# A fused two-block transformer kernel: the first step of both MLPs' down product as seven half-size products, and other row statistics at the border into block 3

## The chip, the cores and the metric

One core of a Trainium2 chip runs the whole kernel in one launch. The metric is the device time of one execution in microseconds (us). Engines: TensorE (PE) multiplies, ScalarE (ACT), VectorE (DVE) and GpSimd (POOL) work on elements, SyncE (SP) issues most DMAs. Each engine takes its instructions in the written order and waits on semaphores.

## The reference, cut to what matters

512 tokens of width 1024 in float32 go through two layers (sparse attention, then gated linear attention, each followed by an MLP) and a third block ("block 3": attention beside an mLSTM, then a gated feed-forward part with adaptive scale and shift). What the change touches:

```python
h = layer_norm(DN_ALPHA * h + mix, ln_mix_g[i], ln_mix_b[i])
h = layer_norm(DN_ALPHA * h + squared_relu_mlp(h, mlp_w_up[i], mlp_w_down[i]), ln_mlp_g[i], ln_mlp_b[i])
# squared_relu_mlp(x, w_up, w_down) = square(relu(x @ w_up)) @ w_down, hidden width 4096
# block 3 begins with modulate(rms_norm(x, norm_mix_g), sh1, sc1) @ w_in
```

## The kernel before, in words

**Precision.** A float32 operand is split into a high half (a rounded copy, `fp32r`, made by ScalarE) and a low half (the difference, made by VectorE, for five chunks by GpSimd). A product is three matmuls: high x high, high x low, low x high.

**Weights** come as chunks of 1 MB into three raw buffers, in the order that `weight_plan` writes; a chunk's halves go to one of the slots 0 to 3. `high(i)` on ScalarE (L1487) waits for the landing and for the last reader of the slot; `low(i)` on VectorE (L2252) waits for `high(i)`. SyncE fetches a chunk when the one three before it has been read (`released`). In between lie 24 conditioning chunks ("ada", 1 MB each), of which VectorE only forms a weighted sum (L2235 for the first of eight, L2238 for the others); the table `ADA` says how many follow each weight of each step. A `Cursor` per engine makes chunks ahead; on VectorE the weight next to a conditioning chunk goes first.

**An MLP** has eight blocks of 512 hidden units. Block n: two up weights, each giving two hidden tiles (128 units x 512 tokens), `gemm_T` (L765 to L767), 96 matmuls; ScalarE takes relu (L1629) and square (L1632) into `rb`. The down product of block n-1 follows the up product of block n. From block 1 on it is a `fold` (L960 to L962): tokens and output columns are halved, and seven products P1 to P7 of half size take the place of eight, 84 matmuls. Their operands are four quadrants of `rb`: P1, P2, P4 take them as they are (P4 the one of hidden tiles 2 and 3, second half of the tokens), the other four take sums that GpSimd makes in place (`hidden_sums`, L3407 to L3415), once the low halves of P1, P4, P2 exist. ScalarE copies each (`high_of`, L1619), VectorE makes the low half (`low_half_of`, L2437). The weights are X (left columns), Z (right), and two that VectorE sums up in the raw buffers (`weight_sums`, L2451 to L2456, and `last_weight_sum`, L2464): Y and W. TensorE's order is P1, P2, P6, P5, P7, P4, P3; P1 and P2 use X, P6 and P4 use Y, P5 uses W, P7 and P3 use Z. P1, P6, P7 are one chain in a PSUM bank, added to `h` on the way (`added`, L2477); P4 and P5 stay in four banks of their own through all steps and are added once (`lasting`); the right lower corner is corrected by the left one before and after (`corner`, L2504).

**Block 0's down product** is a plain one (`down_first`, L986 to L988, 96 matmuls) with its own operand copies (L1645, L2522), and its add also scales `h` by ALPHA (L2513). Beside it VectorE applies the layer norm's gain and shift to the four row tiles, eight pieces (`affine`, L2353).

The queues of the first MLP step of VectorE, as written:

```python
for i in range(4):      # low half of hidden tile i, then affine piece i
    ...
for q in range(2):      # low half of an up weight, then two affine pieces
    ...
cur.take(low)
low_half_of(key, 1, P4)
down_first(0)
```

**The border into block 3** (after the second MLP): TensorE runs block 7's down product by rows (L789 to L791) and, in the middle of the last row, turns rows 0 and 1 (L807); then four `queries` products (L1280 to L1282), with rows 2 and 3 turned in between (L825). VectorE adds each row (L2425), takes `bn_stats` (L2295) and `bn_aggr` (L2906), centres and multiplies by the gain (L2909), scales and shifts (L2915); ScalarE squares the result and takes a root (L1589, L1592), scales it (L1607), and copies the turned quarters (L1530); VectorE splits them (L2288, L2284).

Of the kernel before, what the change touches and what calls it, by code (L numbers as in the profile page):

```python
# [14 lines left out]
P = 128  # L15
# [11 lines left out]
ADA = {0: [(0, 0, 0), (1, 0, 1), (1, 0, 1), (1, 0, 1), (1, 0, 1), (1, 0, 1), (1, 1, 1), (1, 1, 1)],  # L27
       1: [(0, 0, 0), (1, 1, 1), (0, 0, 1), (0, 0, 1), (0, 0, 1), (0, 0, 1), (0, 0, 1), (0, 0, 0)]}
# [176 lines left out]
def weight_plan(a_w_in, a_w_o, b_w_in, b_w_o, mlp_w_up, mlp_w_down, w_ada_2, w_in_2, w_out_2, w_gate_2, w_up_2, w_down_2):  # L205
# [65 lines left out]
    def plan_mlp(i):  # L271
        plan_up(i, 0)
        slots(2, 3, 0, 1)
        plan_up(i, 1)
        for c in range(2):
            plan(mlp_w_down[i], 0, 4, c * 512, 512)
            plan_adas((ADA[i][1][2] + 1 - c) // 2)
        for n in range(2, 8):
            own = 0 if n % 2 else 2
            slots(own, 3)  # L280
# [62 lines left out]
def program(nc, x, positions, a_w_in, a_w_o, b_w_in, b_w_a2, b_b_a, b_g_norm, b_w_o, ln_mix_g, ln_mix_b,  # L343
# [4 lines left out]
    with ctx:  # L348
# [110 lines left out]
        pool_low = (5, 6, 7, 8, 9)  # L459
# [112 lines left out]
        STEPS = {"m1": (1, 6), "m2": (1, 6), "m3": (0, 3)}  # L572
# [16 lines left out]
        def freed(key, d, s):  # L589

            if key == "m3" and (d == 0 or d == 1 and s == P4):
                return s_gemm.at(("o3", T - 1, 1))
            if key != "m3" and d == 1:
                return s_gemm.at((key, "u read", 0)) if s in FIRST else s_gemm.at(None)
            return s_gemm.at((key, "P", d - 2, s, 1)) if s == P4 else s_gemm.at((key, "P", d - 1, s, 1))
# [97 lines left out]
        def tensor_program(pe):  # L693
# [82 lines left out]
            def panel_row(key, hi, lo, k0, ready, nk, first, i, t, cs=(0, 1), amid=None):  # L776
                for c in cs:
# [6 lines left out]
                    for k in range(nk):  # L784
                        if amid and (c, k) == (1, nk // 2):
                            amid()
# [187 lines left out]
            def down_first(key):  # L974
                for c in range(2):
                    i = cur.take(skip)
                    H, L, nk, ncol = parts(i)
                    w.wait_ge(*low_of(i))
                    w.wait_ge(*s_xlow.at((key, "u", 0)))
                    for t in range(T):  # L980
                        name = ((key, "down", 0), t, c)
                        o = bank[banks.take(name)][:, :]
                        w.wait_ge(*banks.free(name, s_act.sem))
                        for f in range(4):
                            X, Y = (v[:, FIRST[f], t * P:(t + 1) * P] for v in (UH4, UL4))
                            pe.matmul(o, X, H[:, f, :], start=f == 0, stop=False)  # L986
                            pe.matmul(o, X, L[:, f, :], start=False, stop=False)
                            step = pe.matmul(o, Y, H[:, f, :], start=False, stop=f == 3)  # L988
                        step.then_inc(*s_gemm.up(name, *([("chunk", i)] if t == T - 1 else [])))
                s_gemm.mark((key, "u read", 0))  # L990

            def mlp(key, x_key):
                for n in range(1, 8):
                    for q in range(2):
                        gemm_T((key, "up", n, q), x_key)
                    if n == 1:
                        down_first(key)
                    else:
                        fold(key, n - 1)
# [254 lines left out]
            def turn_first():  # L1254
                for t in range(2):
                    turn_row("x4", t, xn(t), s_act.at(("xn", t)))
# [203 lines left out]
        def scalar_program(act):  # L1460
# [137 lines left out]

            def roots_next(key):
# [21 lines left out]
            def mlp(key):  # L1621
                def relu(n, q, j):
                    i = 2 * q + j
                    w.wait_ge(*s_gemm.at(((key, "up", n, q), j)))
                    if n == 1:
                        w.wait_ge(*s_xlow.at((key, "u4", 0, i)))
                    elif n > 1:
# [14 lines left out]
                for i in range(4):  # L1642
                    relu(0, i // 2, i % 2)
                    w.wait_ge(*s_act.at((key, "square", 0, i)))
                    act.activation(UH4[:, FIRST[i], :], rb[:, i, :], ACT.Copy).then_inc(*s_xhigh.up((key, "u", 0, i)))  # L1645
                for q in range(2):
                    cur.take(high)
                    relu(1, q, 0)
                    relu(1, q, 1)
                cur.take(high)  # L1650
                high_of(key, 1, P4)
                high_of(key, 1, P1)
                high_of(key, 1, P2)
                cur.take(high)
                for n in range(2, 8):
# [22 lines left out]
                    else:  # L1678
# [3 lines left out]
                        last_high(2)  # L1682
                        weights(q1)
                        last_high(3)
# [529 lines left out]
        def vector_program(dve):  # L2214
# [251 lines left out]
            def mlp(key, x_key, n_gb):  # L2466
                last = {(t, c): ((key, "down", 0), t, c) for t in range(T) for c in range(2)}
# [5 lines left out]
                def into(t, c, ps, name):  # L2473
# [3 lines left out]
                    dve.tensor_tensor(hv, hv, ps, ALU.add).then_inc(*s_row.up(name, ((key, "down", 6), t, c)))  # L2477
# [21 lines left out]
                def corner(t, op, name):  # L2499

                    hv = h[:, t, 512:1024]
                    w.wait_ge(*s_row.at(last[t, 0]))
                    w.wait_ge(*s_row.at(last[t, 1]))
                    dve.tensor_tensor(hv, hv, h[:, t, 0:512], op).then_inc(*s_row.up(name, ((key, "down", 6), t, 1)))  # L2504
                    last[t, 1] = name

                def down_first(c):
                    for t in range(T):
                        name = ((key, "down", 0), t, c)
                        hv = h[:, t, c * 512:(c + 1) * 512]  # L2510
                        w.wait_ge(*s_gemm.at(name))
                        w.wait_ge(*s_row.at((x_key, "h", t)))
                        dve.scalar_tensor_tensor(hv, hv, ALPHA, bank[banks.of[name]][:, :], ALU.mult, ALU.add).then_inc(*s_row.up(name))  # L2513
                        banks.read[name] = s_row.at(name)
# [5 lines left out]
                for i in range(4):  # L2520
                    w.wait_ge(*s_xhigh.at((key, "u", 0, i)))
                    dve.tensor_tensor(UL4[:, FIRST[i], :], rb[:, i, :], UH4[:, FIRST[i], :].bitcast(F), ALU.subtract).then_inc(  # L2522
                        *s_xlow.up((key, "u4", 0, i), (key, "u", 0)))
                    affine(x_key, i, n_gb)
                for q in range(2):
# [3 lines left out]
                cur.take(low)  # L2529
                low_half_of(key, 1, P4)  # L2530
                down_first(0)
                low_half_of(key, 1, P1)
                low_half_of(key, 1, P2)
                cur.take(low)
                down_first(1)
                owed()
# [1116 lines left out]
```

## Time and profile before

| | us |
|---|---|
| median of 3 runs | 1813.71 (1813.1 to 1814.01) |
| the profiled execution | 1814.24, its span 1812.4 |
| TensorE busy | 1780.1 (98%) |
| VectorE, ScalarE, GpSimd busy | 1279.4, 860.4, 251.6 |
| mean granted TensorE clock | 0.998 of full |

Times in the rows below are us from the start of the span, durations are us in timelines and ns where a column says mean ns. A matmul row's 0.39 us is its whole way through the array; the next one starts after 0.227 us. A number in brackets is the engine's idle time before the instruction, and behind it what it waited for.

### The profile page before, as it was taken

What the parts mean: (1) busy time and instruction counts of PE and PEld (TensorE: products, weight loads), DVE (VectorE), ACT (ScalarE), POOL (GpSimd) and SP (SyncE); (2) the same over time, 40 slices, a digit from 0 to 9 for tenths busy, and PEclk for the clock granted to TensorE, in tenths of its full rate; (3) what the DMA queues carried; (4) which work ended last, traced back from release to release, by engine and by line L of the source; (5) the groups of instructions that cost most, each with busy time, mean ns of one, the idle gap of its engine ahead of it and who ended that gap; (6) DMA issues with size and microseconds to landing.
All of it is one profiled execution on the core that took longest, in us unless ns stands there. A gap on an engine that the chain in (4) does not pass through costs nothing.

```text
span 1812.4 us, 22763 instructions
## 1 busy us (share of the span) xinstructions
PE 1780.1 (98%) x8948; PEld 1452.2 (80%) x8948; DVE 1279.4 (71%) x2069; ACT 860.4 (47%) x1340; POOL 251.6 (14%) x188
## 2 busy tenths in 40 slices
PE   9999999999999999999999999999999999999998
PEld 7775788888888888878888888778756898888886
DVE  4997566987788578476777776987667645564774
ACT  4548453454444543555444544465466453332333
POOL 0241101111210054000111111000012001110101
PEclk9999999999999999999999999999999999999999
DMA  6220404544444122141543334232201422421331
GB/s 218 70 70 31 157 24 163 185 140 139 163 167 160 47 70 70 47 144 42 186 139 116 117 120 136 71 95 93 70 25 60 139 70 70 139 73 67 116 117 47
DMA packets 120059, 189.35 MB, mean 104 GB/s; under 512 B 7800, under 2 KB 72536, under 8 KB 116880
## 3 DMA queue, kind: packets, MB, share of 16 engines
q1 hardware_dynamic: 118416, 182.81, 30.6%
q0 software_dynamic: 1392, 4.82, 0.8%
q8 instruction: 71, 1.16, 0.3%
q14 instruction: 36, 0.29, 0.0%
q10 hardware_dynamic: 144, 0.26, 0.0%
HBM read 185.72 MB, written 2.16 MB: 104 GB/s over the span
## 4 chain that ended last, share of the span: by engine, by line
PE 84%; DVE 10%; ACT 4%; issue 2%; DMA 0%; DVEq 0%; ACTq 0%
PE bank L767 11%; PE bank L765 11%; PE bank L766 11%; PE bank L960 6%; PE bank L962 6%; PE bank L961 6%; PE bank L739 3%; PE bank L741 3%; PE bank L740 3%; PE bank L1049 2%; PE bank L1033 2%; PE bank L1024 2%; DVE gb L2735 2%; PE bank L862 2%; PE bank L863 2%
## 5 line engine op out<-in xcount | busy, mean ns | idle before, releaser
L2252 DVE TENSOR_TENSOR wl<-raw,wh 128x2048 fp32r<-128x2048 f32 (+2 forms) x164 | 362.5, 2213 | 115.9 <-ACT wh L1487 115.7
L1487 ACT ACTIVATE wh<-raw 128x2048 fp32r<-128x2048 f32 x169 | 308.9, 1837 | 254.3 <-PE bank L962 62.3
L765 PE MATMUL bank<-xh,wh 128*128 128x512 f32 (+1 forms) x872 | 340.4, 390 | 0.0
L767 PE MATMUL bank<-xl,wh 128*128 128x512 f32 (+1 forms) x872 | 340.0, 390 | 0.0
L766 PE MATMUL bank<-xh,wl 128*128 128x512 f32 (+1 forms) x872 | 340.0, 390 | 0.0
L765 PEld LDWEIGHTS bank<-xh,wh 128*128 128x128 f32 (+1 forms) x872 | 163.7, 188 | 34.9 <-issue 0.8
L767 PEld LDWEIGHTS bank<-xl,wh 128*128 128x128 f32 (+1 forms) x872 | 163.7, 188 | 34.6
L766 PEld LDWEIGHTS bank<-xh,wl 128*128 128x128 f32 (+1 forms) x872 | 163.7, 188 | 34.4
L960 PE MATMUL bank<-wh,uh 128*128 128x512 f32 x432 | 168.4, 390 | 0.0
L962 PE MATMUL bank<-wh,ul 128*128 128x512 f32 x432 | 168.1, 389 | 0.0
L961 PE MATMUL bank<-wl,uh 128*128 128x512 f32 x432 | 168.1, 389 | 0.0
L2477 DVE TENSOR_TENSOR h<-h,bank 128x512 f32<-128x512 f32 x132 | 86.7, 682 | 80.9 <-PE bank L962 80.9
L739 PE MATMUL bank<-wh,xh 128*128 128x512 f32 (+1 forms) x352 | 138.0, 392 | 0.5 <-DVE wl L2252 0.5
L741 PE MATMUL bank<-wh,xl 128*128 128x512 f32 (+1 forms) x352 | 134.0, 381 | 0.0
L740 PE MATMUL bank<-wl,xh 128*128 128x512 f32 (+1 forms) x352 | 133.9, 380 | 0.0
L1629 ACT ACTIVATE A<-bank 128x512 f32<-128x512 f32 x64 | 38.1, 596 | 158.8 <-PE bank L767 142.6
L3407 POOL TENSOR_TENSOR A<-A 128x512 f32<-128x512 f32 x16 | 22.7, 1417 | 590.7 <-DVE ul L2437 590.7
L960 PEld LDWEIGHTS bank<-wh,uh 128*128 128x128 f32 x432 | 81.1, 188 | 19.2 <-issue 2.5
L962 PEld LDWEIGHTS bank<-wh,ul 128*128 128x128 f32 x432 | 81.1, 188 | 16.8
L961 PEld LDWEIGHTS bank<-wl,uh 128*128 128x128 f32 x432 | 81.1, 188 | 16.9
L1619 ACT ACTIVATE uh<-A 128x512 fp32r<-128x512 f32 x112 | 64.3, 620 | 49.7 <-PE bank L962 23.0
L1581 ACT ACTIVATE A<-bank 128x512 f32<-128x512 f32 (+4 forms) x106 | 51.4, 489 | 71.4 <-PE bank L741 31.9
(413 smaller groups left out, 3431.6 us busy)
## 6 DMA issues: line engine op xcount, KB each, us to landing
raw<-in_mlp_w_up SPq DMA_DIRECT2D x32, 1024.0 KB, 6.0
raw<-in_mlp_w_down SPq DMA_DIRECT2D x32, 1024.0 KB, 5.0
raw<-in_w_ada SPq DMA_DIRECT2D x24, 1024.0 KB, 5.0
raw<-in_b_w_in SPq DMA_DIRECT2D x12, 1024.0 KB, 5.2
raw<-in_w_gate SPq DMA_DIRECT2D x11, 1024.0 KB, 5.4
raw<-in_w_up SPq DMA_DIRECT2D x11, 1024.0 KB, 5.4
raw<-in_w_down SPq DMA_DIRECT2D x11, 1024.0 KB, 5.1
raw<-in_w_in SPq DMA_DIRECT2D x10, 1024.0 KB, 5.1
```

The lines of the kernel that those rows point to most:

```text
L739: pe.matmul(o, X, H[:, k, :], start=kk == 0, stop=False)
L740: pe.matmul(o, X, L[:, k, :], start=False, stop=False)
L741: step = pe.matmul(o, Y, H[:, k, :], start=False, stop=kk == 7)
L765: pe.matmul(o, H[:, k, c], xh[:, k, :], start=k == 0, stop=False)
L766: pe.matmul(o, L[:, k, c], xh[:, k, :], start=False, stop=False)
L767: step = pe.matmul(o, H[:, k, c], xl[:, k, :], start=False, stop=k == 7)
L960: pe.matmul(o, X, H[:, k0 + k, :], start=not begun and k == 0, stop=False, skip_group_check=on)
L961: pe.matmul(o, X, L[:, k0 + k, :], start=False, stop=False, skip_group_check=on)
L962: step = pe.matmul(o, Y, H[:, k0 + k, :], start=False, stop=ends and k == 1, skip_group_check=on)
L1487: act.activation(slots[slot_of[i]][0][:, 0:n], raw_of(i)[:, 0:n], ACT.Copy).then_inc(*s_high.up(i))
L2252: dve.tensor_tensor(L[:, 0:n], raw_of(i)[:, 0:n], H[:, 0:n].bitcast(F), ALU.subtract).then_inc(*s_low.up(i))
L2477: dve.tensor_tensor(hv, hv, ps, ALU.add).then_inc(*s_row.up(name, ((key, "down", 6), t, c)))
```

## The change

Block 0's down product becomes a fold like the others: `down_first` and its operand copies go, the operands of d = 0 are made as those of later steps, GpSimd makes four more sums, VectorE four more weight sums, and the scaling by ALPHA moves into the first add of each quarter of `h`. VectorE's affine pieces stand behind P4's, P1's and P2's low halves, and the last four behind the second up weight. The slots of the weights follow a table (`HOMES`); the step's conditioning chunks are spread otherwise. In the last step of an MLP the last down weight is made later. At the border into block 3 `bn_stats` and `bn_aggr` go: the add also sums the row, ScalarE sums the squares around the mean, the centred row goes to a buffer of its own, rows are turned in both halves of the last row's product, and one weight's low half is made by GpSimd.

```diff
-ADA = {0: [(0, 0, 0), (1, 0, 1), (1, 0, 1), (1, 0, 1), (1, 0, 1), (1, 0, 1), (1, 1, 1), (1, 1, 1)],
-       1: [(0, 0, 0), (1, 1, 1), (0, 0, 1), (0, 0, 1), (0, 0, 1), (0, 0, 1), (0, 0, 1), (0, 0, 0)]}
+ADA = {0: [(0, 0, 0), (1, 0, 0), (1, 0, 1), (1, 0, 1), (1, 1, 1), (1, 0, 1), (1, 1, 1), (1, 1, 1)],
+       1: [(0, 0, 0), (1, 0, 0), (0, 0, 1), (1, 0, 1), (0, 0, 1), (1, 0, 1), (0, 0, 1), (0, 0, 0)]}
+HOMES = [(2, 3, 0, 2, 3), (3, 0, 2, 3, 0), (2, 0, 3, 2, 0), (3, 0, 2, 3, 0), (2, 0, 3, 2, 0), (3, 0, 2, 3, 0), (2, 0, 3, 2, 0)]
     def plan_mlp(i):
         plan_up(i, 0)
-        slots(2, 3, 0, 1)
-        plan_up(i, 1)
...
+        for n in range(1, 8):
+            u0, u1, X, Y, W = HOMES[n - 1]
+            slots(u0, u1)
             plan_up(i, n)
-            plan_fold("m%d" % (i + 1), n - 1, mlp_w_down[i], (n - 1) * 512, (2 - own, 1, own, 3), ADA[i][n][2])
-        slots(2, 3)
+            plan_fold("m%d" % (i + 1), n - 1, mlp_w_down[i], (n - 1) * 512, (X, 1, Y, W), ADA[i][n][2])
+        slots(3, 2)
         plan_down(i, 7)
...
-        pool_low = (5, 6, 7, 8, 9)
+        behind_m2 = folds["m2", 6][3] + 4
+        pool_low = (5, 6, 7, 8, 9, behind_m2)
...
-        STEPS = {"m1": (1, 6), "m2": (1, 6), "m3": (0, 3)}
+        STEPS = {"m1": (0, 6), "m2": (0, 6), "m3": (0, 3)}
...
+            def squares_root(t):
+                w.wait_ge(*s_row.at(("x4", "mean", t)))
+                w.wait_ge(*s_xlow.at(("m2", "u", 7)))
+                w.wait_ge(*s_act.now())
+                act.activation(A[:, 0:1024], h[:, t, :], ACT.Square, bias=mv[:, t, 0:1],
+                               accum_out=mv[:, t, 1:2]).then_inc(*s_act.up(("x4", "sq", t)))
+                w.wait_ge(*s_act.now())
+                act.activation(root[:, 4 + t:5 + t], mv[:, t, 1:2], ACT.Sqrt, bias=epsilon[:, 1:2],
+                               scale=1.0 / D).then_inc(*s_act.up(("x4", "rt", t)))
...
                 for i in range(4):
                     relu(0, i // 2, i % 2)
-                    w.wait_ge(*s_act.at((key, "square", 0, i)))
-                    act.activation(UH4[:, FIRST[i], :], rb[:, i, :], ACT.Copy).then_inc(*s_xhigh.up((key, "u", 0, i)))
...
+                high_of(key, 0, P4)
+                high_of(key, 0, P1)
+                high_of(key, 0, P2)
+                for n in range(1, 8):
...
                         last_high(2)
+                        last_high(3)
                         weights(q1)
-                        last_high(3)
...
             for t in range(2):
-                ln_root("x4", t)
-                rms_sum("m2", t, xn(t), "x4")
+                squares_root(t)
                 if t:
                     rms_row("m2", 0, xn)
-                    rms_row("m2", 1, xn)
-            ln_root("x4", 2)
+                rms_sum("m2", t, xn(t), "x4")
+            rms_row("m2", 1, xn)
             half("x4", 0, CS1, SH1, range(4))
+            squares_root(2)
+            half("x4", 0, CS1, SH1, range(4, 8))
             rms_sum("m2", 2, xn(2), "x4")
-            half("x4", 0, CS1, SH1, range(4, 8))
             rms_row("m2", 2, xn)
-            ln_root("x4", 3)
+            squares_root(3)
...
-                for i in range(4):
-                    w.wait_ge(*s_xhigh.at((key, "u", 0, i)))
...
+                for i, s in enumerate((P4, P1, P2)):
+                    low_half_of(key, 0, s)
                     affine(x_key, i, n_gb)
-                for q in range(2):
-                    cur.take(low)
-                    affine(x_key, 4 + 2 * q, n_gb)
-                    affine(x_key, 5 + 2 * q, n_gb)
...
+                affine(x_key, 3, n_gb)
+                for n in range(1, 8):
                     d = n - 1
                     iX, iZ, iY, iW = folds[key, d]
                     cur.take(low, 0)
                     cur.take(low, 0)
                     ada_sum()
+                    if n == 1:
+                        for i in range(4, 8):
+                            affine(x_key, i, n_gb)
+                        for t in (2, 3):
+                            corner_less(t)
                     for s in (P6, P7, P5, P3):
                         low_half_of(key, d, s)
                     weight_sums(key, d)
...
                         added(d, P7)
-                        weights(q1)
                         last_low(3)
                         for t in (2, 3):
-                            corner(t, ALU.add, (key, "more", t))
+                            corner_more(t)
                         lasting(P4, 2, 0, True)
+                        weights(q1)
                         added(d, P3)
...
+                    dve.tensor_tensor_reduce(hv, hv, bank[banks.of[name]][:, :], 1.0, 0.0, ALU.add, ALU.add,
+                                             stats[:, t, c, 0:1]).then_inc(*s_row.up(name))
...
-            cur.take(low, 2)
+            cur.take(low, 1)
             cur.take(low, 0)
+            last_sums()
+            added(0)
+            centred(0)
...
+            normed(0)
             added(1)
             centred(1)
+            rms_root("m2", 0)
             normed(1)
-            rms_root("m2", 0)
+            added(2, (0,))
             rms_root("m2", 1)
-            added(2)
+            cur.make(low)
+            cur.make(low)
+            added(2, (1,))
             centred(2)
             for k in range(4):
                 split("x4", 0, k)
+            added(3, (0,))
             normed(2)
-            cur.make(low)
-            for k in range(4, 6):
+            for k in range(4, 8):
                 split("x4", 0, k)
             rms_root("m2", 2)
-            for k in range(6, 8):
-                split("x4", 0, k)
-            added(3)
+            added(3, (1,))
             centred(3)
...
             load_two(ln_mix_g[0], ln_mix_b[0])
+            hidden_sums("m1", 0)
...
             load_two(ln_mix_g[1], ln_mix_b[1])
+            hidden_sums("m2", 0)
...
             for d in range(1, 7):
                 hidden_sums("m2", d)
+            low(behind_m2)
```

## Rows read from the trace of the kernel before

**Rows 1.** The page, part 1: span, busy us (share) xinstructions of TensorE and VectorE.

```profile
span 1812.4 us, 22763 instructions
...
PE 1780.1 (98%) x8948; PEld 1452.2 (80%) x8948; DVE 1279.4 (71%) x2069; ACT 860.4 (47%) x1340; POOL 251.6 (14%) x188
```

**Rows 2.** The page, part 4: the chain that ended last.

```profile
PE 84%; DVE 10%; ACT 4%; issue 2%; DMA 0%; DVEq 0%; ACTq 0%
```

**Rows 3.** Timeline of TensorE at four boundaries: start us, us, engine, line, out<-in, count.

```profile
287.86 0.39 PE L986 MATMUL bank<-wh,uh 128*128 128x512 f32 x1
...
309.62 0.39 PE L765 MATMUL bank<-xh,wh 128*128 128x512 f32 x1
...
331.37 0.39 PE L960 MATMUL bank<-wh,uh 128*128 128x512 f32 x1
...
350.41 0.39 PE L765 MATMUL bank<-xh,wh 128*128 128x512 f32 x1
```

**Rows 4.** Timeline of VectorE, first MLP, 255 to 295 us; in brackets idle before and its releaser.

```profile
262.10 0.69 DVE L2522 TENSOR_TENSOR ul<-A,uh 128x512 fp32r<-128x512 f32 x1 [1.11 <-ACT uh L1645]
...
271.56 2.29 DVE L2252 TENSOR_TENSOR wl<-raw,wh 128x2048 fp32r<-128x2048 f32 x1
...
273.77 1.28 DVE L2235 TENSOR_SCALAR A<-raw,small 128x2048 f32<-128x2048 f32 x1
...
274.96 2.48 DVE L2353 TENSOR_TENSOR h<-h,gb 128x1024 f32<-128x1024 f32 x2
...
280.34 2.29 DVE L2252 TENSOR_TENSOR wl<-raw,wh 128x2048 fp32r<-128x2048 f32 x1 [2.90 <-ACT wh L1487]
...
291.22 2.29 DVE L2252 TENSOR_TENSOR wl<-raw,wh 128x2048 fp32r<-128x2048 f32 x1 [6.19 <-ACT wh L1487]
```

**Rows 5.** Timeline of ScalarE: hidden tiles 2 and 3 of MLP 1, tile 2 of MLP 2.

```profile
265.91 0.60 ACT L1629 ACTIVATE A<-bank 128x512 f32<-128x512 f32 x1 [2.02 <-PE bank L864]
...
268.35 0.64 ACT L1632 ACTIVATE A<-A 128x512 f32<-128x512 f32 x1
...
858.44 0.60 ACT L1629 ACTIVATE A<-bank 128x512 f32<-128x512 f32 x1 [2.02 <-PE bank L864]
```

**Rows 6.** Timeline of VectorE, first MLP, second step.

```profile
310.42 1.28 DVE L2504 TENSOR_TENSOR h<-h 128x512 f32<-128x512 f32 x2
...
316.09 2.49 DVE L2437 TENSOR_TENSOR ul<-A,uh 128x512 fp32r<-128x512 f32 x4
...
318.50 2.28 DVE L2252 TENSOR_TENSOR wl<-raw,wh 128x2048 fp32r<-128x2048 f32 x1
...
323.88 1.22 DVE L2451 TENSOR_TENSOR raw<-raw 128x1024 f32<-128x1024 f32 x1 [0.28 <-DMA raw<-in_mlp_w_down]
...
331.08 2.28 DVE L2252 TENSOR_TENSOR wl<-raw,wh 128x2048 fp32r<-128x2048 f32 x1
...
335.50 1.22 DVE L2252 TENSOR_TENSOR wl<-raw,wh 128x1024 fp32r<-128x1024 f32 x1
```

**Rows 7.** Timelines of VectorE and of GpSimd (POOL), where both read SBUF.

```profile
300.75 3.38 DVE L2252 TENSOR_TENSOR wl<-raw,wh 128x2048 fp32r<-128x2048 f32 x1
...
302.06 3.23 POOL L3409 TENSOR_TENSOR A<-A 128x512 f32<-128x512 f32 x1
...
340.56 1.28 POOL L3413 TENSOR_TENSOR A<-A 128x512 f32<-128x512 f32 x1
```

**Rows 8.** The border into block 3: windows (length, TensorE busy), and two timeline rows.

```profile
1148.67:1202.85 54.18, 49.37 (x225) 1.00 0.15 37
...
1154.15 0.69 DVE L2295 BATCH_NORM_STATS2 stats<-h 128x6 f32<-128x512 f32 x1
...
1178.11 1.06 ACT L1589 ACTIVATE A<-h 128x1024 f32<-128x1024 f32 x1 [2.72 <-DVE h L2915]
```

**Rows 9.** GpSimd's groups by line and form: count | busy us, mean ns | idle before.

```profile
L3402 POOL TENSOR_TENSOR wl<-raw,wh 128x2048 fp32r<-128x2048 f32 x5 | 23.1, 4624 | 77.8 <-ACT wh L1487 77.8
```

**Rows 10.** Windows, TensorE: length, busy us (count), granted clock, DMA share, GB/s.

```profile
616.00:622.00 6.00, 6.00 (x19) 0.72 0.19 43
```

More of the change, by code:

```diff
@@ L592, in freed @@
                 return s_gemm.at(("o3", T - 1, 1))
-            if key != "m3" and d == 1:
-                return s_gemm.at((key, "u read", 0)) if s in FIRST else s_gemm.at(None)
+            if d == 0 or d == 1 and s == P4:
+                return s_gemm.at(None)
             return s_gemm.at((key, "P", d - 2, s, 1)) if s == P4 else s_gemm.at((key, "P", d - 1, s, 1))
@@ L784, in panel_row @@
                     for k in range(nk):
-                        if amid and (c, k) == (1, nk // 2):
-                            amid()
+                        if amid and k == nk // 2:
+                            amid(c)
                         w.wait_ge(*ready(k0 + k))
@@ L972, in fold @@
                 ada_turn()
[L974 to L990, printed above, removed]
             def mlp(key, x_key):
@@ L995, in mlp @@
                         gemm_T((key, "up", n, q), x_key)
[L996 to L999, printed above, removed]
+                    fold(key, n - 1)
             scored = []
@@ L1253, in tensor_program, with turn_first @@
             mlp("m2", "x3")
-            def turn_first():
-                for t in range(2):
-                    turn_row("x4", t, xn(t), s_act.at(("xn", t)))
+            def turn_first(t):
+                turn_row("x4", t, xn(t), s_act.at(("xn", t)))
             i = [cur.take(skip, 3), cur.take(skip, 0)]
@@ L2466, in mlp @@
             def mlp(key, x_key, n_gb):
-                last = {(t, c): ((key, "down", 0), t, c) for t in range(T) for c in range(2)}
+                last = {(t, c): (x_key, "h", t) for t in range(T) for c in range(2)}
+                scaled = set()
                 def last_low(i):
@@ L2476, in into @@
                     w.wait_ge(*s_row.at(last[t, c]))
-                    dve.tensor_tensor(hv, hv, ps, ALU.add).then_inc(*s_row.up(name, ((key, "down", 6), t, c)))
+                    if (t, c) in scaled:
+                        dve.tensor_tensor(hv, hv, ps, ALU.add).then_inc(*s_row.up(name, ((key, "down", 6), t, c)))
+                    else:
+                        dve.scalar_tensor_tensor(hv, hv, ALPHA, ps, ALU.mult, ALU.add).then_inc(*s_row.up(name, ((key, "down", 6), t, c)))
+                    scaled.add((t, c))
                     last[t, c] = name
@@ L2497, in lasting, with corner_less, corner_more @@
                             banks.read[where] = s_row.at(name)
-                def corner(t, op, name):
-                    hv = h[:, t, 512:1024]
+                def corner_less(t):
+                    hv, name = h[:, t, 512:1024], (key, "less", t)
+                    w.wait_ge(*s_row.at(last[t, 0]))
+                    dve.tensor_tensor(hv, hv, h[:, t, 0:512], ALU.subtract).then_inc(*s_row.up(name))
+                    last[t, 1] = name
+                def corner_more(t):
+                    hv, name = h[:, t, 512:1024], (key, "more", t)
                     w.wait_ge(*s_row.at(last[t, 0]))
                     w.wait_ge(*s_row.at(last[t, 1]))
-                    dve.tensor_tensor(hv, hv, h[:, t, 0:512], op).then_inc(*s_row.up(name, ((key, "down", 6), t, 1)))
+                    dve.scalar_tensor_tensor(hv, hv, ALPHA, h[:, t, 0:512], ALU.mult, ALU.add).then_inc(
+                        *s_row.up(name, ((key, "down", 6), t, 1)))
+                    scaled.add((t, 1))
                     last[t, 1] = name
[L2507 to L2514, printed above, removed]
                 def owed():
@@ L2902, in centred @@
+                    banks.read[name] = s_row.at(name)
+            centre = A[:, 1024:2048]
             def centred(t):
-                hv = h[:, t, :]
                 w.wait_ge(*s_row.now())
-                dve.bn_aggr(mv[:, t, :], stats[:, t, :, :].rearrange("p a b -> p (a b)")).then_inc(*s_row.up(("x4", "mv", t)))
+                dve.tensor_scalar(mv[:, t, 0:1], stats[:, t, 0, 0:1], stats[:, t, 1, 0:1], -1.0 / D, ALU.add,
+                                  ALU.mult).then_inc(*s_row.up(("x4", "mean", t)))
@@ L2907, in centred @@
                 w.wait_ge(s_gb, 16 * G_M2)
                 w.wait_ge(*s_row.now())
[L2909 removed]
+                dve.scalar_tensor_tensor(centre, h[:, t, :], mv[:, t, 0:1], gb[:, 0:D], ALU.add, ALU.mult).then_inc(*s_row.up())
             def normed(t):
[L2912 to L2913 removed]
+                w.wait_ge(*s_act.at(("x4", "sq", t)))
```

51 lines of the change are left out of this document (8 added, 43 removed).

## The prediction, made before the changed kernel was seen to run

> **What bounds the kernel now.** I read the page's busy times first: TensorE is busy for 1780 of 1812.4 us [rows 1]. The chain that ended last says the same: 84% TensorE, 10% VectorE [rows 2]. So work taken from TensorE pays in full only if nothing else becomes late, and I went next to TensorE's own timeline around the first down step of the first MLP [rows 3]. There matmuls follow each other at 0.227 us without a hole: block 1's old first down step runs from 287.86 to 309.62 (21.76 us for 96 matmuls), and the next step, which is already done with seven products, from 331.37 to 350.41 (19.04 us for 84). The counts of matmuls are those of the code: 4 row tiles x 2 column halves x 4 k x 3, and 7 x 2 x 2 x 3.
>
> The profiled execution took 1814.24 us (span 1812.4 and 1.8 around it); the median is 1813.71. I work out differences against the former and put them on the latter. A change under 0.2% (3.6 us) can't be told from none.
>
> **The change, part by part.**
>
> *The products.* 96 matmuls become 84 in each MLP: 12 x 0.227 = 2.72 us, twice 5.44 us. This is TensorE time without cover, so it counts in full if its operands are there in time.
>
> *Whether they are there.* The fold needs, in this order: at its start the low halves of X and of P1's operand; 5.4 us later those of Y, which comes out of four sums on VectorE; 8.2 us later W's. Today's starting time would be 287.86. All of them stand in VectorE's queue, so I lay that queue out for MLP 1.
>
> Today VectorE uses the time while ScalarE finishes the hidden tiles: from 262.1 on it does a low half and an affine row piece by turns [rows 4]. In the new order its first instruction there is P4's low half. P4 reads hidden tiles 2 and 3, so it waits for ScalarE's square of tile 3 (start 268.35, 0.64 us, [rows 5]) and P4's copy behind it; one 0.63 us copy (tile 2's) goes from ahead of that square and P4's comes. The low half starts at 269.1, and VectorE has been idle for 8 us: the affine pieces that filled that hole are queued behind.
>
> Then, without a pause, by the starts in [rows 4, 6]: 3 low halves (0.62) 1.9; 4 affine pieces (1.24) 5.0; low half of the second up weight 2.2; conditioning product 1.2; 4 affine pieces 5.0; two corner subtractions 1.2; 4 low halves 2.5; X's low half 2.3. Sum 21.2: X is there at 290.3. (One conditioning chunk of 2.34 leaves this step in MLP 1, two in MLP 2; that is in the list already.) The up weight in this list is late too: at 278.2 where TensorE wants it at 276.98 (48 matmuls ahead of 287.86).
>
> *GpSimd's four sums.* Today they meet VectorE while it mostly adds out of PSUM. Where they meet an SBUF instruction the rows are plain [rows 7]: VectorE's low half that takes 2.29 alone took 3.38 from 300.75, and ended 2.15 us after GpSimd's sum had; the next GpSimd sum, begun at 302.06, took 3.23 in place of 1.30 and ended 1.16 us after that low half. Each waits for the other's whole instruction, and GpSimd gets in between two of VectorE's: about 1.05 us lost to VectorE per sum. In the new step the four sums start when P1's low half is done (271.6), into an unbroken run of two-input SBUF instructions. Bounds: nothing (no meeting), or 4 x 1.05 = 4.2; the queue has no gap there, so I take 4.2. The Trainium skill (SBUF - State Buffer, section Who interferes with whom) says that a VectorE instruction with two SBUF inputs and a GpSimd instruction reading SBUF exclude each other for the whole instruction; taken at its word it would cost 4 x 1.30 = 5.2, one more than the rows. By these rows the trace agrees.
>
> So X at 294.5. From there to Y's low half the queue of the present second step gives 9.5 us (323.88 to 333.36, [rows 6]): 304.0. To W's low half come two adds, a low half and 1.22: 3.05, so 307.0. TensorE then has four products of 2.72 left: it ends at 317.9, where the old step ended at 309.62. **Per MLP: +8.3 us** (in time it would end at 287.86 + 19.04 = 306.9; so 11.0 of lateness, 4.2 of it by the blocking, against 2.7 saved), and +4.1 without the blocking. Behind it the add of P7, which frees the bank of the next up product, follows an up low half and a conditioning chunk and is done about when that bank is wanted: 0 to 0.3. From the second step on the queue has today's order, and today has 3.4 us to spare at Y (333.36 against 336.8): no stall.
>
> MLP 2 has the same queues, and its hidden tile 2 comes at 858.44 as the first one's at 265.91 [rows 5]: +8.3 again, 16.6 in all, with bounds 8.2 and 17.
>
> *Moved and re-homed things, costed at nothing.* X and Z stay in their raw buffers until the sums are over, so SyncE's fetches of the next up weights and conditioning chunks go out behind them; a landing takes 5 to 6 us and the next step's first use is 10 us off. If that cover is gone, a fetch costs its landing. In the second step the first up weight takes W's slot, free after the fourth product: 8.2 us remain for 4.2 us of halves. The last down weight takes Y's slot, free after the sixth product: 5.4 us for 4.2, so 1.2 to spare; if not, some tenths of a us at each border. The conditioning chunks moved to later steps join steps like the present sixth and seventh, which carry three without a stall.
>
> *The border into block 3.* From 1148.67 to 1202.85 TensorE is busy for 49.37 of 54.18 us [rows 8]: 4.8 us is the most to be had. The holes are waits for the chain column add, bn_stats, centre, norm, square, scale, turn. The change takes 8 bn_stats (0.69) off VectorE, of which the four of rows 2 and 3 (2.8) stand on that chain, and the low half of a weight (2.29). It puts ScalarE's squares of rows 2 and 3 (1.25 each) into it, partly beside the centring. Two halves of a column add move ahead. The GpSimd low half takes 4.62 [rows 9] and starts at 1152.7, so row 0's centring (two SBUF inputs, due at 1155.2) is held until 1157.3: 2.1 us, most of it absorbed since row 3 is what TensorE waits for. Bounds: -4.8 and +2. I take 5.1 - 2.5 + 0.6 (the moved halves) = **-3.2 us**.
>
> **Sum:** +16.6 - 3.2 = +13.4: 1827.6 for the profiled one, 1827.0 for the median. The first border keeps its order and is costed at nothing.
>
> **The rivals.**
>
> *On the other side: VectorE's queue is in time and the products pay.* It would need X's low half by 287.9 and Y's by 293.3. For it: VectorE has idle time in this stretch now (2.9 us before 280.34, 6.2 before 291.22, [rows 4]), and TensorE has no hole there. It decides at the start of the first low half: were that at 262 and not 269, X would come at 283 to 287. Against it: the written order, in which P4 stands first on both engines. Time 1813.7 - 5.4 - 3.2 = 1805.
>
> *Late, but without the blocking.* The sums fall on instructions that don't exclude them. 2 x 4.1 - 3.7 = +4.5: 1818. Against it: rows 7. A mix of the two lies between.
>
> *The stall also costs clock.* TensorE would stand still for some 5 us before the second up weight and 4 before P6. The granted clock fell once in the trace, behind a few matmuls of only 16 rows: from 616 to 622 it was 0.72 on average [rows 10], which is to say partly at 1.2 in place of 2.4 GHz, and 6 x 0.28 = 1.7 us were lost. Where TensorE waits for VectorE again right after, it is hidden; after P6 it is not: +1.7 per MLP, 1830.5.
>
> *The products don't save what they should* would leave today's 21.76 us; the 19.04 us of each later step speaks against it, and I give it nothing.
>
> **How the numbers follow.** Late with blocking 0.55 (1822 to 1829), late with lost clock 0.12 (1829 to 1832), late without blocking 0.18 (1815 to 1821), in time 0.15 (1803 to 1808). The likeliest gives 1827. The range leaves out the case in time and the top of the clock case: 1815 to 1831. Faster by over 0.2%: 0.14. Within: the low end of the third case and the top of the fourth, 0.11. Slower: 0.75.
>
> **What would show it.** TensorE waiting for VectorE's weight low half (L2252) in the middle of the first up product of each MLP, some 5 us, and again before P1 (1) and P6 (4); VectorE idle for 8 us ahead of the first low half of each MLP and then full for 35; affine pieces and up low halves 1 us longer than alone, GpSimd's sums 2 to 3 us. The fold itself still 84 matmuls. At the border four squares on ScalarE and no bn_stats, first query product about as early as now and the last one 3 us earlier. It would be wrong if those waits are under 1 us, or if the affine pieces run ahead of the first low half.

## The result, and the profile after

The changed kernel takes 1829.49 us (median of 4 runs, 1828.1 to 1831.56) where the kernel before, beside it, takes 1813.86: a ratio of 1.0084, 95% interval 1.0072 to 1.0097, so 0.8% slower. The prediction was 1827.0, range 1815 to 1831, slower with 0.75. The profiled execution took 1830.58 us, its span 1828.8: 16.4 more than the span before.

The page's part 1 (busy times) and the engines' shares of the chain that ended last, after; they answer to [rows 1, 2]:

```profile
PE 1782.8 (97%) x8924; PEld 1453.9 (80%) x8924; DVE 1303.9 (71%) x2090; ACT 874.0 (48%) x1358; POOL 273.4 (15%) x197
...
PE 82%; DVE 12%; ACT 4%; issue 2%; DMA 0%; DVEq 0%; ACTq 0%
```

24 matmuls are gone, as they should be, and yet TensorE is busy for 2.7 us longer: some matmuls ran at a lower clock (rows below). VectorE's share of the chain rose from 10 to 12%.

TensorE's timeline in the first MLP, at the wait in the middle of block 1's up product, at the fold's start, at the wait before P6 and at the next up product; it answers to [rows 3]:

```profile
276.67 0.39 PE L765 MATMUL bank<-xl,wh 128*128 128x512 f32 x1
281.98 0.80 PE L763 MATMUL bank<-xh,wh 128*128 128x512 f32 x1 [4.92 <-DVE wl L2229]
...
294.83 0.39 PE L958 MATMUL bank<-wh,uh 128*128 128x512 f32 x1
...
300.05 0.39 PE L960 MATMUL bank<-wh,ul 128*128 128x512 f32 x1
303.86 0.76 PE L958 MATMUL bank<-wh,uh 128*128 128x512 f32 x1 [3.42 <-DVE h L2458]
...
320.34 0.39 PE L763 MATMUL bank<-xh,wh 128*128 128x512 f32 x1
```

A hole is counted here from the start of one matmul to the start of the next, which are 0.227 us apart where there is none. Two holes of 5.3 and 3.8 us stand where the prediction had them. Up product and first down step take 54.35 us together (265.99 to 320.34) in place of 43.55: +10.8. In the second MLP it is 53.21, +9.7. The windows are those of the kernel before (MLP 1, 43.55 in MLP 2 too) and, after, of MLP 2 (length, then TensorE, its loads, VectorE, ScalarE and GpSimd busy, granted clock, DMA share, GB/s):

```profile
266.07:309.62 43.55, 43.55 (x195) 36.04 (x194) 28.17 (x24) 19.46 (x23) 8.52 (x6) 1.00 0.51 169
```

```profile
869.26:922.47 53.21, 45.27 (x183) 36.47 (x182) 44.73 (x40) 26.90 (x32) 14.62 (x10) 0.90 0.34 114
```

All the other folds still take 19.04 us or within 0.2 of it. The second hole ends on something that the prediction had not named: not on Y's low half but on `L2458`, VectorE's add of P1 right behind it.

VectorE's timeline beside this, for [rows 4, 6], and GpSimd's four sums, for [rows 7]:

```profile
268.93 0.69 DVE L2414 TENSOR_TENSOR ul<-A,uh 128x512 fp32r<-128x512 f32 x1 [8.00 <-ACT uh L1606]
269.54 1.22 DVE L2330 TENSOR_TENSOR h<-h,gb 128x1024 f32<-128x1024 f32 x1
...
272.42 1.79 DVE L2414 TENSOR_TENSOR ul<-A,uh 128x512 fp32r<-128x512 f32 x1
274.13 4.52 DVE L2330 TENSOR_TENSOR h<-h,gb 128x1024 f32<-128x1024 f32 x2
278.58 3.35 DVE L2229 TENSOR_TENSOR wl<-raw,wh 128x2048 fp32r<-128x2048 f32 x1
...
291.44 2.28 DVE L2229 TENSOR_TENSOR wl<-raw,wh 128x2048 fp32r<-128x2048 f32 x1
...
300.83 2.29 DVE L2229 TENSOR_TENSOR wl<-raw,wh 128x2048 fp32r<-128x2048 f32 x1
303.03 1.28 DVE L2458 SCALAR_TENSOR_TENSOR h<-h,bank 128x512 f32<-128x512 f32 x2
```

```profile
271.45 2.21 POOL L3387 TENSOR_TENSOR A<-A 128x512 f32<-128x512 f32 x1 [71.47 <-DVE ul L2414]
273.74 1.61 POOL L3389 TENSOR_TENSOR A<-A 128x512 f32<-128x512 f32 x1
275.49 2.08 POOL L3393 TENSOR_TENSOR A<-A 128x512 f32<-128x512 f32 x1
277.65 2.12 POOL L3395 TENSOR_TENSOR A<-A 128x512 f32<-128x512 f32 x1
```

VectorE idles for 8.00 us, then has no gap. Beside GpSimd a low half takes 1.79 and not 0.69, two affine pieces 4.52 and not the 2.48 of [rows 4], the up weight's low half 3.35 and not 2.29: 1.1 + 2.04 + 1.06 = 4.2 us lost. X's low half (291.44) ends at 293.7, Y's (300.83) at 303.1.

TensorE's clock, from the windows view (the granted clock is the third number from the end), for [rows 10]; the windows begin or end at the two holes, and the last line is a stretch that begins in the first hole:

```profile
265.99:276.67 10.68, 10.68 (x50) 8.82 (x48) 7.70 (x7) 7.47 (x9) 5.00 (x3) 1.00 0.00 0
276.67:281.98 5.31, 0.39 (x3) 0.00 (x1) 5.31 (x3) 2.30 (x4) 3.03 (x2) 0.73 0.00 0
281.98:294.60 12.62, 12.62 (x47) 10.28 (x48) 12.55 (x13) 2.35 (x4) 1.10 (x2) 0.84 0.76 251
...
303.86:315.00 11.14, 11.14 (x37) 8.97 (x38) 6.54 (x10) 2.90 (x3) 5.47 (x4) 0.73 0.59 188
...
320.34:342.10 21.76, 21.76 (x98) 18.02 (x96) 19.44 (x15) 11.39 (x13) 0.00 (x0) 1.00 0.31 115
...
279.10:285.93 6.83, 3.95 (x9) 3.15 (x10) 6.79 (x5) 0.81 (x2) 0.68 (x1) 0.50 0.21 58
```

From each hole on the clock is at 1.2 in place of 2.4 GHz for a while (0.50 on average from 279.10 to 285.93). And the border into block 3, for [rows 8], from the first matmul of block 7's down product to that of the product behind the queries, with GpSimd's low half and the centring beside it:

```profile
1168.98:1219.96 50.98, 48.35 (x225) 38.84 (x223) 40.39 (x107) 38.77 (x73) 5.74 (x3) 1.00 0.18 45
```

```profile
1173.11 4.63 POOL L3382 TENSOR_TENSOR wl<-raw,wh 128x2048 fp32r<-128x2048 f32 x1 [50.64 <-ACT wh L1463]
```

```profile
1175.68 3.13 DVE L2888 SCALAR_TENSOR_TENSOR A<-h,mv,gb 128x1024 f32<-128x1024 f32 x1
```

The same stretch took 54.81 before: -3.8.

```profile
1148.67:1203.48 54.81, 49.52 (x225) 38.51 (x223) 45.21 (x109) 33.39 (x65) 1.11 (x2) 1.00 0.14 37
```

So +10.8 + 9.7 - 3.8 = 16.7, and the span grew by 16.4.

### The profile page after: what moved, and what is told of

The parts are those of the page before. It is cut to its first block, busy times and chain, and to the rows that moved or that the text cites. A ratio compares the mean times of both kernels' runs of the same rounds, so it can differ in the third digit from the quotient of the medians.

```text
span 1828.8 us, 22776 instructions
## 1 busy us (share of the span) xinstructions
PE 1782.8 (97%) x8924; PEld 1453.9 (80%) x8924; DVE 1303.9 (71%) x2090; ACT 874.0 (48%) x1358; POOL 273.4 (15%) x197
## 4 chain that ended last, share of the span: by engine, by line
PE 82%; DVE 12%; ACT 4%; issue 2%; DMA 0%; DVEq 0%; ACTq 0%
PE bank L763 10%; PE bank L765 10%; PE bank L764 10%; PE bank L958 6%; PE bank L959 6%; PE bank L960 6%; PE bank L737 3%; PE bank L739 3%; PE bank L738 3%; DVE wl L2229 2%; PE bank L1026 2%; PE bank L1010 2%; PE bank L1001 2%; DVE gb L2707 2%; PE bank L860 2%
## 5 line engine op out<-in xcount | busy, mean ns | idle before, releaser
L2229 DVE TENSOR_TENSOR wl<-raw,wh 128x2048 fp32r<-128x2048 f32 (+1 forms) x167 | 367.7, 2204 | 106.3 <-ACT wh L1463 106.2
L1463 ACT ACTIVATE wh<-raw 128x2048 fp32r<-128x2048 f32 (+2 forms) x173 | 314.5, 1829 | 253.4 <-PE bank L960 68.4
L958 PE MATMUL bank<-wh,uh 128*128 128x512 f32 x488 | 192.4, 394 | 6.4 <-DVE h L2458 6.4
L959 PE MATMUL bank<-wl,uh 128*128 128x512 f32 x488 | 191.6, 393 | 0.0
L960 PE MATMUL bank<-wh,ul 128*128 128x512 f32 x488 | 191.3, 392 | 0.0
L958 PEld LDWEIGHTS bank<-wh,uh 128*128 128x128 f32 x488 | 92.6, 190 | 29.0 <-DVE wl L2229 7.2
L960 PEld LDWEIGHTS bank<-wh,ul 128*128 128x128 f32 x488 | 92.7, 190 | 19.5
L959 PEld LDWEIGHTS bank<-wl,uh 128*128 128x128 f32 x488 | 92.7, 190 | 19.2
L2414 DVE TENSOR_TENSOR ul<-A,uh 128x512 fp32r<-128x512 f32 x126 | 87.9, 738 | 20.2 <-ACT uh L1606 20.1
L1606 ACT ACTIVATE uh<-A 128x512 fp32r<-128x512 f32 x126 | 72.2, 620 | 59.0 <-POOL A L3393 24.4
```

The source lines that it names most:

```text
L958: pe.matmul(o, X, H[:, k0 + k, :], start=not begun and k == 0, stop=False, skip_group_check=on)
L959: pe.matmul(o, X, L[:, k0 + k, :], start=False, stop=False, skip_group_check=on)
L960: step = pe.matmul(o, Y, H[:, k0 + k, :], start=False, stop=ends and k == 1, skip_group_check=on)
L1463: act.activation(slots[slot_of[i]][0][:, 0:n], raw_of(i)[:, 0:n], ACT.Copy).then_inc(*s_high.up(i))
L2229: dve.tensor_tensor(L[:, 0:n], raw_of(i)[:, 0:n], H[:, 0:n].bitcast(F), ALU.subtract).then_inc(*s_low.up(i))
```

## Experiments

A ratio is to the kernel before on the same chip.

**e1: the border alone**, put into the kernel before.

> The kernel before with only the change at the border into block 3. Theory: the border stage takes 51.0 us from the first row to the end of the queries in the changed kernel and 54.8 in the one before (-3.8), whatever the products do, so 1810.0 us. Rival: the gain there is lent by the late start of the stage (other fetches have landed by then); then this kernel stays at 1813 to 1814.

Measured: 1810.22, ratio 0.9982 (0.9972 to 0.9992), the stretch 50.96 us: as expected. **e2: the products alone**, the changed kernel with the old border.

> The changed kernel with the border as it was before. Theory: the two first steps cost +10.8 and +9.7 us, nothing else: 1813.9 + 20.4 = 1834.3, and one measurement cross-checks e1 (the two parts should add up to the changed kernel's +15.6 within 1 us). Rival: the parts depend on each other, the sum is off by more than 2 us.

Measured: 1833.0, ratio 1.0107 (1.0092 to 1.0122), 1.3 us under what was expected. The two parts don't depend on each other within the noise: -0.18 and +1.07% make +0.89, against +0.84 for both.

**e9: the border alone, its low half on VectorE again.** The edit as against the changed kernel's border:

```diff
-        pool_low = (5, 6, 7, 8, 9, behind_m2)
+        pool_low = (5, 6, 7, 8, 9)
```

> e1 (the kernel before with the change's border) with the low half at the border on VectorE again and not on GpSimd: the squares and the half column adds alone. Theory of the prediction: GpSimd's low half takes 2.3 us off VectorE and holds row 0's centring for 1.9 us, so it is worth next to nothing by itself; the squares on ScalarE bring the gain: 0.9985 of before (0.9978 to 0.9992), within 1 us of e1. Rival: the low half is the larger part of the gain: 0.9995 to 1.0005. Rival on the other side: the held centring costs more than the low half gives: 0.9970 or less.

Measured: 0.9986 (0.9977 to 0.9995), the stretch 51.46 us. The centring is back at 1.29 us from e1's 3.15, and the low half's 2.2 us are on VectorE again, later. So the low half on GpSimd is worth 0.5 us in the profiles (one of each kernel), which the times can't tell from nothing. The other changes at the border bring the rest, some 3.3 us, all together: sums and squares in place of `bn_stats`, the moved half adds, the centred row's own buffer and the earlier turns. No run tells these apart. The two stretches, e1 and e9:

```profile
1149.94:1200.90 50.96, 48.36 (x225) 38.85 (x223) 39.21 (x108) 38.71 (x73) 5.74 (x3) 1.00 0.15 38
```

```profile
1149.89:1201.35 51.46, 48.22 (x226) 38.86 (x224) 39.53 (x109) 38.77 (x73) 1.11 (x2) 1.00 0.15 39
```

**e3: four affine pieces in VectorE's 8 us of idleness**, ahead of P4's low half, the rest unchanged.

```diff
-                for i, s in enumerate((P4, P1, P2)):
-                    low_half_of(key, 0, s)
-                    affine(x_key, i, n_gb)
-                affine(x_key, 3, n_gb)
+                for i in range(4):
+                    affine(x_key, i, n_gb)
+                for s in (P4, P1, P2):
+                    low_half_of(key, 0, s)
```

> The changed kernel with the first four affine pieces ahead of P4's low half, in VectorE's idle 8 us, and nothing else moved. Theory (VectorE's queue is what makes TensorE wait): no wait before the second up weight, a short one before P1, and some 5 us before P6; per MLP 5 to 6 us less, so 1818 us (1816 to 1820). Rival (VectorE's load, or the fold itself, and not the order sets the time): the same instructions are there, so 1828 or more.

Measured: 1822.22, ratio 1.0047 (1.0032 to 1.0062). The direction holds, some 4 us are missing. The up product no longer waits in the middle (23.12 us with the wait before P1), but before P6 there is still a hole of 4.7 us, and in each MLP the clock is at half for 6.8 us from that hole on. Up product and down step take 49.28 us in MLP 1 and 49.67 in MLP 2, 5.1 and 3.5 less than in the changed kernel. The two windows of MLP 1:

```profile
266.82:289.94 23.12, 21.95 (x98) 17.84 (x96) 19.07 (x17) 12.14 (x17) 10.24 (x6) 1.00 0.41 137
289.94:316.10 26.16, 21.82 (x84) 17.55 (x85) 21.78 (x21) 12.29 (x12) 5.48 (x4) 0.87 0.34 110
```

**e4: six pieces ahead, the last two and the corner subtractions behind the third new low half** (and P7's add ahead of the next conditioning chunk; the edit is cut to its middle).

```diff
+                        for i in (6, 7):
+                            affine(x_key, i, n_gb)
+                        for t in (2, 3):
+                            corner_less(t)
                         added(d, P6)
...
```

> The changed kernel with VectorE's first step put in another order: six affine pieces in the idle 8 us, the last two and the two corner subtractions behind P2's low half of the next step, and P7's add ahead of the next conditioning chunk. Theory: X's low half comes at 283 and Y's at 292, P6 waits under 1 us for P1's add, so the products pay their 5.4 us and the border its 3.8: 1805 us (1804 to 1807), faster than both kernels. Rival (the GpSimd sums and the load keep it late): 1815 or more.

Measured: 1815.93, ratio 1.0013 (1.0004 to 1.0023): a miss by 11 us. Up product, P1, P2, P6 and P5 run in time now (P6 is 0.4 us late), but P7 waits. TensorE's row, and VectorE's behind which it stands:

```profile
302.82 0.50 PE L958 MATMUL bank<-wh,uh 128*128 128x512 f32 x1 [3.15 <-DVE h L2458]
```

```profile
298.49 2.47 DVE L2330 TENSOR_TENSOR h<-h,gb 128x1024 f32<-128x1024 f32 x2
300.88 1.29 DVE L2485 TENSOR_TENSOR h<-h 128x512 f32<-128x512 f32 x2
302.08 1.28 DVE L2458 SCALAR_TENSOR_TENSOR h<-h,bank 128x512 f32<-128x512 f32 x2
```

P1, P6 and P7 collect in the same banks (`CHAIN`), and the fold waits, ahead of P6 and P7, for VectorE's add of the one before. I had put 3.6 us of other work (298.49 to 302.08) ahead of P6's add.

**e5: P6's add first.** From e4, with one affine piece moved into a wait for ScalarE (after the conditioning product; that line is left out here):

```diff
-                            for i in (6, 7):
-                                affine(x_key, i, n_gb)
+                            added(d, P6)
+                            affine(x_key, 7, n_gb)
                             for t in (2, 3):
                                 corner_less(t)
-                            added(d, P6)
```

> The order of e4, but with VectorE's add of P6 directly behind the third new low half, and one affine piece, and the two corner subtractions after it (another affine piece goes to VectorE's pause after the conditioning product). Theory: what held e4 up was TensorE's P7 waiting for the add of P6 on the bank that the two share (3.5 us), and the half clock behind that wait (1.7 us); both go, the seven products of each MLP take 19.0 to 19.7 us, and the time is 1806 (1804 to 1808). Rival: P7 isn't what was late but the next bank or the hidden sums on GpSimd, and the wait only moves on: 1813 to 1816.

Measured: ratio 0.9956 (0.9943 to 0.9970), 1808.72 against 1815.89 on its chip, which is 1805.7 by the 1813.71 of before. As expected, and the fastest of all: 0.44% below the kernel before, 1.3% below the changed one. The interval is wide, 5.4 to 10.3 us below the kernel before; the profiles' rows make 6.6: 3.8 at the border and 1.39 in each MLP (42.16 in place of 43.55), about half of the 2.72 that the twelve matmuls are worth. Its up product and first down step (the first two windows, MLP 1; the last is MLP 2's down step), at full clock:

```profile
266.72:288.51 21.79, 21.79 (x99) 18.03 (x97) 19.78 (x16) 14.07 (x18) 9.16 (x4) 1.00 0.29 97
288.51:308.88 20.37, 19.28 (x85) 15.69 (x84) 20.34 (x21) 10.42 (x11) 6.37 (x4) 1.00 0.57 183
...
880.41:900.77 20.36, 19.28 (x85) 15.69 (x84) 18.85 (x21) 12.31 (x12) 6.23 (x5) 1.00 0.55 184
```

Of the 1.33 us above 19.04 that are left, 1.25 are P6's wait for P1's add (its first matmul starts 1.48 us behind the one before it, not 0.227).

**e8: that wait too.** From e5, W's sum behind the add of P1.

```diff
-                    last_weight_sum(key, d)
+                    if n > 1:
+                        last_weight_sum(key, d)
                     weights(iY)
...
                     added(d, P1)
                     if n < 7:
+                        if n == 1:
+                            last_weight_sum(key, d)
                         low_half_of(key, n, P4)
```

> e5 with the last weight sum of the first step (W's, 1.23 us) behind VectorE's add of P1 and not ahead of Y's low half. Theory: in e5 P6 still waits 1.26 us, for Y's low half and the add of P1 right behind it; both come 1.2 us earlier, W's low half some 0.6 us later than P5 would like it: the fold takes 19.1 to 19.8 us in place of 20.37, and the time is 0.5 to 1.2 us per MLP below e5's: 0.9944 of before (0.9935 to 0.9952). Rival: P5 becomes the one that waits, for W, by as much as P6 is spared: the fold stays at 20.4 and the ratio at 0.9956.

Measured: 0.9987 (0.9978 to 0.9996), a miss, and worse than the rival had it. ScalarE's timeline shows why:

```profile
292.19 0.63 ACT L1617 ACTIVATE A<-A 128x512 f32<-128x512 f32 x1
295.34 1.06 ACT L1463 ACTIVATE wh<-raw 128x1024 fp32r<-128x1024 f32 x1 [2.51 <-DVE raw L2441]
296.30 1.65 ACT L1606 ACTIVATE uh<-A 128x512 fp32r<-128x512 f32 x3
```

W's copy is ahead of the next three operand copies in ScalarE's queue; all wait for the later sum, and VectorE, next in line with P4's low half, idles for 1.64 us. P5 then waits 2.1 us for W. The folds take 21.83 us in MLP 1 and 23.14 in MLP 2, where 3.4 us of half clock follow the wait.

**e6: GpSimd's four sums done by VectorE** behind its third low half, in the changed kernel.

```diff
+                sums0()
                 affine(x_key, 3, n_gb)
```

`sums0` is the four instructions of `hidden_sums`, written for VectorE; those of later steps stay on GpSimd.

> The changed kernel with the four hidden sums of the first step done by VectorE itself, behind its third low half, and not by GpSimd. Theory: GpSimd's four sums cost VectorE 4.2 us by exclusion and the same sums cost VectorE 4 x 0.65 = 2.6 us when it does them itself, so X comes 1.6 us earlier, and each MLP ends 1.5 to 2 us earlier, with a little less clock lost: 1826 (1824 to 1827). Rival: the affine pieces are slow for another reason (their own access of memory) and stay at 2.2 us, the sums add to them: 1833 to 1835.

Measured: 1828.97, ratio 1.0074 (1.0061 to 1.0088), against 1.0084: lower, by less than the intervals; by the 1813.71 of before it is 1827.1, just above what was expected. So the reading rests on the trace. An affine piece takes 1.22 us again and the up weight's low half 2.29:

```profile
274.08 1.22 DVE L2330 TENSOR_TENSOR h<-h,gb 128x1024 f32<-128x1024 f32 x1
...
278.06 1.22 DVE L2330 TENSOR_TENSOR h<-h,gb 128x1024 f32<-128x1024 f32 x1
279.20 2.29 DVE L2229 TENSOR_TENSOR wl<-raw,wh 128x2048 fp32r<-128x2048 f32 x1
```

Counted from the up product's start, X's low half ends at 26.2 and not 27.7; TensorE's wait for the up weight is 3.4 and not 4.9 us. Up product and down step take 52.6 and 51.7 us, against 54.35 and 53.21: 3.2 us back in the two MLPs. The span fell by 1.4 only, for the half clock behind the small matmuls near 626 (the place of [rows 10]) lasted 6.8 us here and 3.4 in the changed kernel's profile.

**e7: TensorE kept at work in its two holes**, with transposes whose results are written over.

```diff
+                if key[1:] == ("up", 1, 1):
+                    b = banks.order[0]
+                    w.wait_ge(*banks.read.get(banks.user[b], (s_act.sem, 0)))
+                    for _ in range(38):
+                        pe.transpose(bank[b][:, 0:P], ident, ident)
                 w.wait_ge(*low_of(i))
```

and the same with 26 ahead of P6's waits.

> The changed kernel with TensorE kept at work in its two long waits of the first step (38 transposes ahead of the wait for the second up weight, 26 ahead of the wait before P6, into the bank that is taken next; their results are written over). Nothing that it waits for comes earlier. Theory: the half clock that followed the waits was set off by TensorE standing still; the 6.8 us stretches are gone and the second MLP's too, which gives back some 3 us in the first MLP and 1.7 in the second: 1824 to 1826. Rival: the clock falls at this place for another reason (the load of the matmuls themselves): the stretches stay, and the time is 1829 to 1830, or above it by what the transposes cost.

Measured: 1827.92, ratio 1.0068 (1.0054 to 1.0082); by the 1813.71 of before it is 1826.0, the upper end of what was expected. The windows of up product and down step, MLP 1, then MLP 2:

```profile
266.11:293.94 27.83, 26.43 (x137) 21.98 (x135) 24.77 (x21) 12.13 (x17) 9.15 (x6) 1.00 0.36 110
293.94:317.86 23.92, 22.42 (x111) 18.52 (x111) 21.84 (x20) 12.42 (x12) 5.52 (x4) 1.00 0.37 114
868.51:896.32 27.81, 26.40 (x136) 21.97 (x134) 24.76 (x21) 12.12 (x17) 9.15 (x6) 1.00 0.34 113
896.32:920.13 23.81, 22.31 (x110) 18.68 (x111) 20.72 (x20) 14.75 (x15) 5.51 (x4) 1.00 0.35 111
```

Full clock throughout, though VectorE is as late as before: in MLP 1 P6 starts 37.90 us behind the up product's start, and 37.87 in the changed kernel. 51.75 and 51.62 us are 2.6 and 1.6 us less than in the changed kernel, and in MLP 1 all of it comes behind P6's start (13.85 us in place of 16.48). That is the clock's part, and it comes from TensorE standing still. The time fell by less than the 4.2 of the two MLPs (2.3 in the span), again with 6.8 us of half clock near 624 in place of 3.4.

## Why the prediction was right, point by point

**Products and border.** 84 matmuls in place of 96, as said. The border was -3.2 predicted, -3.8 in the trace and -3.3 by e1's ratio, but the terms of that sum don't hold, and that it came out near is luck. It had 2.29 us for the low half that leaves VectorE and 0.9 (2.8 - 2.5 + 0.6) for everything else; e1 and e9 have 0.5 for the low half and 3.3 for everything else. GpSimd's low half began at 4.1 us into the stretch and held row 0's centring for 1.84 us, where I had 4.0 and 2.1; the 0.5 has this hold in it.

**VectorE's queue.** First low half at 269.1 predicted, 268.93 measured; idle 8 and 8.00; up weight ready at 282.4 (278.2 + 4.2) and 281.9; X at 294.5 and 293.7; Y at 304.0 and 303.1. Of the 0.8 at X, 0.2 is the start and most of the rest the affine pieces, which the list has at 1.24 (half of a row of two) and which start 1.14 to 1.20 apart.

**The blocking.** 4.2 us predicted, 4.2 in the rows. e6 takes it away: X 1.5 us earlier, about the 4.2 less the 2.8 (275.2 to 278.1) in which VectorE now does the sums itself. The Trainium skill (SBUF — State Buffer, section Who interferes with whom) has the shared port as an exclusive lock for the whole instruction; the trace agrees in kind: the gaps cost VectorE 1.02 to 1.10 us for each GpSimd sum, less than the 1.30 that one takes alone.

**Per MLP +8.3.** With full clock (e7) it is 51.75 and 51.62 against 43.55: +8.2 and +8.1. P1's wait, predicted at 1 us, is 0.8 there.

**What failed: the chance of the clock case.** The prediction had the mechanism, its place (behind P6, hidden before it) and nearly its size (+1.7 per MLP) as a rival with 0.12, and left it out of the likeliest case. It happened in both MLPs: +2.6 and +1.6, and 1829.49 lies in that rival's band (1829 to 1832), not in the likeliest one's (1822 to 1829). That is the whole difference between 13.4 predicted and 16.3 measured for the profiled execution (4.2, less 0.6 at the border, 0.3 in the MLPs' sums and 0.3 elsewhere in the kernel). The prediction says that the clock fell once in the trace of before, behind small matmuls [rows 10], and I took it for an oddity. It fell twice. The second time was at the end, 2.6 us after TensorE's last matmul had ended (1805.65), with TensorE idle:

```profile
1805.65:1808.23 2.58, 0.00 (x1) 0.00 (x0) 2.24 (x5) 1.49 (x4) 0.00 (x0) 1.00 0.49 200
1808.23:1812.43 4.20, 0.00 (x0) 0.00 (x0) 1.02 (x4) 0.72 (x1) 0.00 (x0) 0.50 0.34 129
```

It costs nothing there, but the forecast waits of 5 and 4 us are longer than those 2.6, and the row speaks for a higher chance than 0.12. The lower clock also hid a little: the slow second half of the up product took 12.85 us in place of 10.88, and so P1's own wait, predicted at 1 us, isn't there.

**What was overlooked: the bank chain.** "Y 304.0" was taken as P6's condition; P6 also waits for the add of P1 behind it (+0.6). Here it was small. It decided e4, whose expectation has P1's add ahead of P6 but not P6's add ahead of P7: listing what each product of the chain waits for would have shown on paper that P7 is late.

**The rival in time** was right in what it asks for and wrong in its sign. e5 has X's low half at 285.1 (it asked for 287.9) and Y's at 294.5 (293.3, in e5's time 293.9), and reaches 0.9956, or 1805.7, where the case in time had 1805. But its first low half starts at 269.67 and not at 262: what decides is how much of the other work stands ahead of that low half, not when it starts.

**Slips in the sums.** The case without the blocking takes -3.7 at the border, where the sum has -3.2; with -3.2 it is 1818.7 and not 1818. The clock case is 1827.0 + 2 x 1.7 = 1830.4, not 1830.5. Neither moves a bound.

## What to carry to other kernels

Twelve matmuls fewer per MLP helped only once the queues that feed them were laid out again: when a step is put in the place of another, list for each product all its conditions, operands and the bank's earlier reader alike, and for each wait what stands behind it on its engine (e4, e8). Work that filled an engine's idle time must stay ahead of the wait when the order is rewritten: with four of the eight affine pieces back in it and nothing else moved (e3), up product and down step of MLP 1 are 5.1 us shorter (49.3 against 54.4). And price a hole on TensorE of the size seen here (3 to 5 us) with the half clock behind it, not with its length alone, unless another wait right behind takes that up (as before P6 here).

## What the runs showed of the hardware beyond what was expected

- All 16 holes of 3.1 to 5.3 us on TensorE, in five kernels, were followed by a stretch of half clock of 3.4 or 6.8 us, which began in the hole or up to 1.5 us behind its end. Holes of 1.5 us (e3, e5) had none. The hole of 2.5 us before P5 in e8 had none behind it in MLP 1 and 3.4 us in MLP 2. With transposes in the holes (e7) there was none.
- The half clock behind the small matmuls between 615 and 627 lasted 0 (e2, e4), 3.4 (before, after, e1, e8, e9) or 6.8 us (e3, e5, e6, e7) in one profile each; 3.4 us at half clock cost 1.7.
- Beside GpSimd a VectorE instruction with a single tensor as input was slower too: the conditioning product took 2.32 us in e4, from 274.45, beside GpSimd's sums, and 1.28 in the changed kernel, from 281.85, with GpSimd idle.
